# A two-block transformer kernel: 27 groups of 2x2 blocks of the down-projections made with seven block products instead of eight

## What is computed

```python
def sq_relu_mlp(h, w1, w2):
    return jnp.square(jax.nn.relu(h @ w1)) @ w2
...
    up = causal_dwconv(h @ w_up[l], conv_w[l], conv_b[l])
    y = (jax.nn.gelu(up[..., :D_FF_2], approximate=True) * up[..., D_FF_2:]) @ w_down[l]
    x = x + rms_norm_2(y, post_ffn_g[l])
```

## Time and profile before

| | |
|---|---|
| runs | 2095.36 us median (2094.35 to 2097.16) |
| profiled execution | 2095.49 us, span 2093.8 us |
| granted TensorE clock | 0.999 |
| TensorE busy | 2083.5 us, 9304 matmul records |
| TensorE weight loads | 1728.1 us, beside the matmuls |
| VectorE busy | 1224.2 us |
| ScalarE busy | 1072.2 us |
| POOL busy | 119.7 us |
| HBM read | 432.75 MB, 223 GB/s with the writes |

### The profile page before, as it was taken

The page is one execution under the profiler, slowest core; times in us unless marked ns, Lnnn a source line. Parts: engine busy times, 40 slices in busy tenths (PEclk is TensorE's granted clock), DMA queues, the critical chain, the costliest instruction groups (busy, mean ns, idle before and its releaser), DMA issues.

```text
span 2093.8 us, 23749 instructions
## 1 busy us (share of the span) xinstructions
PE 2083.5 (100%) x9304; PEld 1728.1 (83%) x9304; DVE 1224.2 (58%) x1312; ACT 1072.2 (51%) x1303; POOL 119.7 (6%) x66
## 2 busy tenths in 40 slices
PE   9999999999999999999999999999999999999998
PEld 8888888888888888888888888888888888888887
DVE  6546556655554555455566755566666654566665
ACT  7555654555434543455455554455555533555553
POOL 3000000000000000000002000000112100011120
PEclk9999999999999999999999999999999999999999
DMA  8688666888667885688588777667878766787863
GB/s 297 197 251 236 191 188 216 260 248 235 211 193 206 241 254 194 196 243 238 192 270 232 229 244 232 197 203 211 249 236 250 220 211 193 223 247 242 251 221 121
DMA packets 291903, 469.46 MB, mean 224 GB/s; under 512 B 18512, under 2 KB 82128, under 8 KB 291280
## 3 DMA queue, kind: packets, MB, share of 16 engines
q1 hardware_dynamic: 290928, 463.46, 72.5%
q10 hardware_dynamic: 864, 4.49, 0.6%
HBM read 432.75 MB, written 35.13 MB: 223 GB/s over the span
## 4 chain that ended last, share of the span: by engine, by line
PE 96%; DVE 1%; DMA 1%; ACT 1%; issue 0%; SPq 0%; ACTq 0%; DVEq 0%
PE ps L1546 96%; DMA T<-passed_strip 1%; DVE Wl L1204 0%; DVE zs L1416 0%; ACT Wh L986 0%; DMA E<-passed_rows 0%; DVE T L1256 0%; DMA gains<-in_gains_dram 0%; DVE E L1416 0%; ACT zs L1125 0%; SPq L917 0%; DMA passed_rows<-xN 0%; ACT T L1044 0%; DVE aHL L1307 0%; PE ps L1549 0%
## 5 line engine op out<-in xcount | busy, mean ns | idle before, releaser
L1204 DVE TENSOR_TENSOR Wl<-raw,Wh 128x1024 fp32r<-128x1024 f32 x743 | 908.2, 1242 | 674.2 <-ACT Wh L986 673.6
L1546 PE MATMUL ps<-Wh,aHL 128*128 128x512 f32 x3712 | 1148.8, 390 | 2.4 <-DVE Wl L1204 0.8
L986 ACT ACTIVATE Wh<-raw 128x1024 fp32r<-128x1024 f32 x743 | 768.0, 1054 | 611.1 <-PE ps L1546 608.7
L1546 PEld LDWEIGHTS ps<-Wh,aHL 128*128 128x128 f32 x3712 | 696.8, 188 | 147.9 <-DVE Wl L1204 1.3
L1546 PE MATMUL ps<-Wl,aHL 128*128 128x512 f32 x1856 | 722.1, 389 | 0.0
L1546 PE MATMUL ps<-Wh,hid 128*128 128x512 f32 x1728 | 532.8, 389 | 0.0
L1546 PEld LDWEIGHTS ps<-Wl,aHL 128*128 128x128 f32 x1856 | 348.4, 188 | 71.8
L1546 PEld LDWEIGHTS ps<-Wh,hid 128*128 128x128 f32 x1728 | 324.3, 188 | 67.4
L1546 PE MATMUL ps<-Wl,hid 128*128 128x512 f32 x864 | 336.1, 389 | 0.0
L1546 PEld LDWEIGHTS ps<-Wl,hid 128*128 128x128 f32 x864 | 162.2, 188 | 33.7
L1546 PE MATMUL ps<-Wh,oHL 128*128 128x512 f32 x512 | 159.0, 390 | 0.0
(11 more groups left out here) (167 smaller groups left out, 687.4 us busy)
## 6 DMA issues: line engine op xcount, KB each, us to landing
raw<-in_mlp_w_dram SPq DMA_DIRECT2D x256, 512.0 KB, 4.5
raw<-in_w_up_dram SPq DMA_DIRECT2D x176, 512.0 KB, 4.6
raw<-in_sb_w_qkv_dram SPq DMA_DIRECT2D x93, 512.0 KB, 5.2
raw<-in_w_down_dram SPq DMA_DIRECT2D x88, 512.0 KB, 4.7
raw<-in_w_in_dram SPq DMA_DIRECT2D x64, 512.0 KB, 4.8
passed_strip<-T SPq DMA_DIRECT2D x104, 256.0 KB, 4.5
T<-passed_strip SPq DMA_DIRECT2D x208, 128.0 KB, 5.2
raw<-in_sb_w_o_dram SPq DMA_DIRECT2D x32, 512.0 KB, 5.4
```

The costliest lines, as they stand in the source:

```text
L986: e.activation(Wh[:, i % NW, :], rawv[:, i % NRAW, :], ACT.Copy).then_inc(st["hi"][0], 1)
L1204: e.tensor_tensor(Wl[:, i % NW, :], rawv[:, i % NRAW, :], Wh[:, i % NW, :].bitcast(F32), ALU.subtract).then_inc(st["lo"][0], 1)
L1546: return e.matmul(o, l, r, start=start, stop=stop, skip_group_check=True)
```

## The change

In 15 places of the first block's down-projection and 12 of the second's, a 2x2 block of weights (two K tiles, even and odd, of two neighbouring strips a and b) and the matching 2x2 block of tokens (rows 0 and 1, even and odd tile) are multiplied by a Winograd form of Strassen's method: seven block products for eight. A group stands in the list as four pieces, s0 to s3, of two, two, two and one products (6, 6, 6 and 3 matmuls), in place of two pieces of 12. Only s0 and s1 load weights. Four sums of weights are made on VectorE (`weight_sums`), two of them then split as s2 and s3. Four sums of tokens are made once per pair of tiles, three pairs a chunk (`mix_tokens`, `mix_low`), into a new buffer hidMix. Four of the seven products, summed over the chunk's three groups, gather in ps2, three go straight to ps0 and ps1; at the pair's end `fold` and `fold_rest` add the four banks into the rows.

The first group comes after 4 plain pieces (2 in a pair without a tail), with 3 plain pieces between groups (2 in the second pairs of the chunks of five). The last pair of the first block has none. The first block's tokens now carry r before the square (a scale in the relu), so its sums are added plainly. In the second block the hid halves are planned 3 pieces on instead of 2.

```diff
+        b[0]["first"], b[0]["start"] = False, (False, True)
+        lead, gap = (4, 3) if tail else (2, 3 if len(plain) > 7 else 2)
+        rest = a[lead:n] + b[:n] if tail else a[lead:n - 1] + b[:2] + a[n - 1:] + b[2:]
+        p.pieces[first:] = a[:lead]
+        for m, kp in enumerate(sevens):
+            seven(w, s4, kp, mov, tiles, (a[0]["strip"], b[0]["strip"]), koff, m, m == 0, fold if m == len(sevens) - 1 else None)
+            p.pieces += rest[gap * m:gap * m + gap] if m < len(sevens) - 1 else rest[gap * m:]
+        p.pieces += a[n:] + b[n:] if tail else []
...
+    def mix_tokens(mov, src, k, n, need):
+        d = [done("token_mixed") for c in range(4)]
+        hi, lo = done("mixed_hi"), done("mixed_lo")
+        step("mix_tokens", mov=mov, src=src, k=k, n=n, need=[*need, *free["sums"]], d=d, hi=hi)
+        free["sums"] = [lo]
+        later(1, lambda: step("mix_low", mov=mov, k=k, n=n, hi=hi, lo=lo))
...
-            trip(s, k, n, "relu", None, [], landed)
+            trip(s, k, n, "relu", "b", [st["r2"]], landed)
...
                     step("gate_halves", t0=t0, need=[g, *k], hi=hi, lo=lo)
                     free["E"] = [lo]
+                    if t0 < 8:
+                        free["E"] = [lo, mix_tokens("hid2", "E", t0 // 2, 2 if t0 == 0 else 1, [g])]
...
-                later(2, halves)
+                later(3, halves)
...
+        q, n = p.pieces[i], int(p.pieces[i]["kind"][1])
+        if n == 0:
+            made = {m: done("weights_added") for m in (1, 3, 2, 4)}
+            step("weight_sums", a=raw_of[i] % NRAW, b=raw_of[i + 1] % NRAW, need=[landed(i), landed(i + 1), *free["sums"]], made=made)
+            free["sums"] = [(lo_sem, i + 4)]
+            for m in (1, 2, 3):
+                p.pieces[i + m]["made"] = made[(3, 2, 4)[m - 1]]
+        step("split", i=i, part=q["kind"], slot=raw_of.get(i, 0) % NRAW, loaded=landed(i) if n == 0 else q["made"],
+             used=(mm_sem, i - NW + 1), hi=(hi_sem, i + 1), lo=(lo_sem, i + 1))
+        if i in raw_of:
+            load(raw_of[i] + NRAW)
...
+                elif k == "weight_sums":
+                    e.tensor_tensor(wsum[:, 0, :], a[:, 0, :], b[:, 0, :], ALU.add).then_inc(made[1][0], 1)
+                    e.tensor_tensor(b[:, 0, :], b[:, 0, :], b[:, 1, :], ALU.add).then_inc(made[3][0], 1)
+                    e.wait_ge(*made[1])
+                    e.tensor_tensor(wsum[:, 1, :], wsum[:, 0, :], b[:, 1, :], ALU.add).then_inc(made[2][0], 1)
+                    e.wait_ge(*made[2])
+                    e.tensor_tensor(wsum[:, 2, :], wsum[:, 1, :], a[:, 1, :], ALU.add).then_inc(made[4][0], 1)
...
+            def seven_products(q):
+                terms = {"s0": (("a11", side[:, 0, :], q["opens"], True), ("a12", a[:, 0, :], False, False)),
+                         "s1": (("d1", side[:, 2, :], q["opens"], True), ("d3", b[:, 0, :], q["opens"], False)),
+                         "s2": (("d0", side[:, 1, :], q["opens"], True), ("d2", side[:, 3, :], q["opens"], True)),
+                         "s3": (("a22", a[:, 1, :], False, False),)}[q["kind"]]
+                for t, (name, P, starts, ends) in enumerate(terms):
+                    c = slice(t * 512, (t + 1) * 512)
+                    x, h, l = halves_of[name]
+                    mm(P, x[:, h:h + 128], wh[:, c], starts, False)
+                    mm(P, x[:, h:h + 128], wl[:, c], False, False)
+                    m = mm(P, x[:, l:l + 128], wh[:, c], False, ends and q["closes"])
```

231 lines of the change are left out of this document (178 added, 53 removed).

## The result

The changed kernel takes **2122.43 us** (median of 4 runs, 2117.78 to 2124.08) where the kernel before takes 2096.26 (4 runs, 2094.35 to 2098.72): 1.0121 times as long, 95% interval 1.0100 to 1.0141. 2097.0 had been forecast, with a range up to 2102.5. The profiled execution is the shortest of the four, 2117.78 us, span 2116.0. It is 22.2 us longer than the span before (2093.8), although TensorE has 81 matmuls fewer.

What follows compares the result with a forecast made beforehand. TensorE was taken as the bound, busy 2083.5 of 2093.8 us. Terms of -18.4 + 14.3 + 4.6 + 0.5 + 0.4 = +1.4 us gave 2097.0 us, range 2089.5 to 2102.5.

Steps and rivals of the forecast that it cites:

- the starts of the second block: From its down-projections' first piece (T0), piece 16's remainder comes 7.6 and 6.7 us late: 14.3 us, bounds 10.3 and 15.4.
- mixing: Second block's up-projections: token sums ahead of a strip's turn cost 3.45 us, two more places 0.6 each: 4.6, bounds 2 and 6.
- the remainder behind it is 4 us early: A fold falls where plain pieces follow, so the next remainder on VectorE is still 4 us ahead of need.
- the last down-projection: Squares of a finished strip stand on ScalarE before a group's third piece, 0.4 us late; bounds 0 and 2.
- saving: 27 groups make 21 matmuls of 24 each: 81 fewer at 0.2267 us, 18.4 us, all on the path.
- rival 2: The clock falls in the new gaps at the second block's down-projection starts: 8.6 us more, 2105.6 us; chance 0.25.
- first block's down-projections: At their three starts piece 11's remainder is 0 to 1.0 us late: 0.5 us for the three, bounds 0 and 3.
- A group among others costs nothing: Groups between plain pieces: VectorE's added sums fit, with a least cover of 2.2 us.
- That the halves come one piece later changes nothing here: it is POOL they wait for: Second block's down-projection starts: planning the halves 3 pieces on adds nothing to the chain from turn to piece 16.
- rival 1: The reload comes sooner and the second block's waits shrink: 2090.3 us; with everything hidden 2077; chance with everything hidden 0.25.
- the likeliest case: The forecast itself, 2097.0 us, within 0.2% of no change; chance 0.50.

Runs made afterwards that it cites:

- experiment 7: Changed kernel cut to 20 groups: none in the second block's tail pairs, two in the first block's third chunk; mixing 6 pieces behind halves at 2: 2093.15 us.
- experiment 12: Kernel of experiment 10 (17 groups) with halves 2 pieces on instead of 3 and mixing 7 pieces behind them instead of 6: 2085.22 us.
- experiment 10: Kernel of experiment 9 (18 groups) with two groups instead of three in the very last pair, so 17 groups: 2086.50 us.
- experiment 4: Changed kernel, all 27 groups, with the second block's token mixing planned 6 pieces after the halves: 2108.65 us.
- experiment 11: Kernel of experiment 4 with the weight sums of the second block's groups made over 8 columns instead of 512: 2102.0 us.
- experiment 3: Changed kernel without the second block's groups; the first block's 15 groups, token mixing and later halves stay: 2103.4 us.
- experiment 2: Kernel of experiment 1 with the three groups of the first block's third chunk back in, so 15 groups: 2090.17 us.
- experiment 1: Changed kernel with only the 12 groups of the first block's chunks 1 and 2; no second-block groups or mixing, halves 2 pieces on: 2087.01 us.
- experiment 8: Kernel of experiment 7 with one more group in each tail pair of the second block, behind 8 and 7 plain pieces: 2109.59 us.
- experiment 9: Kernel of experiment 7 without the first block's third-chunk groups, halves at 3 and mixing 6 behind, so 18 groups: 2087.91 us.
- experiment 13: Kernel before the change with only the second block's halves 3 pieces on instead of 2, no group, no mixing: 2096.29 us.

## Why the prediction was wrong

The profiled span was to grow by 1.4 us and grew by 22.2. Four terms of the sum were too small: the starts of the second block (the last strip's reload was taken to go out at T0 + 12.0, and POOL's product to keep its length), mixing (costed at three places), the first block's third down-projection ("the remainder behind it is 4 us early"), and the last down-projection (the bank, and the fold ahead of the last rounding). The table has the terms of the sum. A wait is a distance of two matmul starts over 0.62 us, less 0.227, and the row of the clock is the excess of the shorter distances:

| term | forecast | measured |
|---|---|---|
| saving | -18.4 | -18.4 |
| waits at the two starts in the second block | 14.3 | 15.9 (7.9, 8.0) |
| matmuls at the lower clock, there and behind | 0 (rival 2: 8.6) | 8.2 (2.3, 3.7, and 2.2 from 2057 on) |
| mixing in the up-projections | 4.6 | 8.0 (6.7, 1.25) |
| first block's down-projections | 0.5, at the starts | 3.8, at the end of the third |
| rest of the last down-projection | 0.4 | 4.6 |
| sum | 1.4 | 22.1 |

**The saving** and **"A group among others costs nothing"** were right. Two down-projections of the first block show it (18 matmuls fewer, 4.08 and 4.05 us), and so do second pairs of the second block where nothing else is in the way: 1.9 and 1.7 us for 9 matmuls in the first down-projection of experiments 7 and 12, 1.4 us for 6 in the last one of experiments 10 and 12.

**The starts of the second block** were right in mechanism: TensorE waited before pieces 11, 12 and 16, for a chain of fixed length. Their size was not, since waits and slow matmuls together made piece 16 later than forecast. Times from T0, first and second down-projection:

| | forecast | measured |
|---|---|---|
| reload issued | 12.0, 10.9 | 13.6, 14.3 |
| from there to the turn | 8.9 | 9.3, 10.2 |
| turn to the end of piece 16's remainder | 17.9 | 18.5, 18.4 |
| TensorE late at piece 16 | 7.6, 6.7 | 10.1, 11.7 |

(By the prediction's own steps the second is 6.5, not 6.7; the difference is small.) The step that failed is the first row. The chain was started too early: the convolution of the strip before was put at T0 + 7.0, as in the trace of before, and ended at T0 + 8.3 and 9.0; the reload stands behind it, by way of piece 5's remainder. The step "That the halves come one piece later changes nothing here: it is POOL they wait for" hid 1.1 us of that in each: POOL's product for the strip before is itself 1.13 us longer for the remainder that now stands ahead of the halves. The last strip's product is longer by 0.6, which is the third row. A wait before piece 4 (1.3 and 1.95 us) was not looked for either: the four sums stand ahead of that piece's remainder, whose cover had been 2.7 us in the first. From the reload's issue to the turn it took 19.5 us in both together, for 18.9 in the earlier trace rows, against rival 1.

**Rival 2, the clock, happened**, at both starts and once more at 2057. But its excess of 8.2 us is not its price. Of it 5.9 us (2.2 and 3.7) ran ahead of the two pieces 16, and those remainders were done 18.4 to 18.5 us behind the turn at all six such starts (the changed kernel, experiments 4 and 11), whether the slow matmuls ahead had cost 1.3 or 3.9 us. TensorE came to piece 16 with its remainder just done (cover 0.06 and 0.05 us), so at full clock it would have waited there instead. What the clock can have cost the span is by this estimate 8.2 - 5.9 = 2.3 us, nearly all of it behind 2057; no run here has these waits with the clock held up. The prediction let such a wait absorb 1.8 us a start, too little. The clock's fall itself was the consequence to expect, given the two waits of some 3 us each with 1.4 us of work between that the prediction derived, and the one row at hand (idle 2.26 us, clock still 1.00 and then 0.60) did not speak against it. So the likeliest case was worth less than its 0.5. Rival 2's 2105.6 would have been nearer, but by a price that was mostly not there, and still 12 us short of the profiled execution.

**Mixing** was costed right where it was looked at (3.45 at the turn) and then as two further places of 0.6. Six waits came in the first chunk, since the cover in these up-projections was down to 1.1 to 2.1 us at each of the next strips too, not at one alone, and every strip starts from a chain that is already late. Experiment 3 puts mixing and halves at 12.2 us in the up-projections alone (against experiment 2), and experiments 4 and 12 show that the whole is a matter of place.

**The first block's third down-projection** was worked out at its start, where the remainder of piece 11 kept 0.44 us of cover (0 to 1.0 late had been forecast), and not at its end. The alternation of VectorE and ScalarE for the norms was in the trace of before, with a cover that fell from 8.3 to 2.1 us; "the remainder behind it is 4 us early" (behind the fold) was taken as harmless, when it was the cover that this stretch lives on. Experiment 2 against 1 shows the loss, 2.0 us net, though 1.1 of its 3.2 us of waits are at the stage's start. That start, forecast as 0 to 1.0 late for each chunk, was on time in all three chunks of the changed kernel and late by 1.1, 1.0 and 3.0 us in the third chunk of experiments 2, 7 and 8: that it was on time here is in part luck.

**The last down-projection**: the squares ahead of a group were seen, but not that a pair's first group already waits for the neighbour strip's bank, behind 2 pieces of the pair where plain pieces open it behind 10, and behind a fold (2.3 us), nor that the last fold delays the last rounding (1.6). Experiment 10 shows the second by removing it. The first is absent in experiments 7, 9, 10 and 12, where the second pair has groups and no fold stands ahead of it; that fits, but it was not tried alone.

What stays open: the second start's chain began 3.0 us later against T0 than before (the turn of the strip before at T0 + 0.3 for T0 - 2.7), of which 1.1 is POOL's. Its other part varies between kernels that are the same up to there (T0 - 0.03 with 18 groups, T0 - 1.16 with 17), so it is at least partly a matter of when the reload lands; no run here separates it from mixing's. Nor is it known what makes the other three executions of the changed kernel 3.6 to 6.3 us longer than the profiled one.

## What to carry to other kernels

Before adding work to an engine that feeds the bottleneck, list the cover of every piece through the program, not the idle time of the engine: VectorE was 58% busy and had room for all the sums, and still the same mixing, with the later halves, cost 8 us in one place and nothing six pieces on. A place that is costed as late must be followed to the end of its stage (what starts from it, what alternates with it, and whether the waits that it makes bring the clock down), and a saving should be put only where the cover has come back: 17 groups of the 27 give 0.54% where all 27 lose 1.2%. The best version here is the one of experiment 12, 2085.2 us.

## What had not been expected of the hardware

**POOL's product takes as long as VectorE lets it.** 128x1024 elements took 5.58 us with three remainders of VectorE beside it and 6.71 with four. Less 1.14 us for each remainder that is 2.16 and 2.15 us: as though POOL stood still while VectorE made its remainders (both read two tiles). Counted by the overlap in the traces, POOL's time less VectorE's beside it is 2.2 to 2.3 us in 154 of the 165 products of all 15 profiles. It can go the other way: in eight of them POOL took 5.58 us, and it was the fourth remainder, begun 0.0 to 0.3 us behind the third, that took 3.0 to 3.4 us for its 1.23 and ended 1.1 behind POOL. Experiment 13's POOL and VectorE:

```profile
1829.74 5.58 POOL L1529 TENSOR_TENSOR E<-E,zs 128x1024 f32<-128x1024 f32 x1 [163.58 <-DVE E L1416]
...
1833.40 3.01 DVE L1204 TENSOR_TENSOR Wl<-raw,Wh 128x1024 fp32r<-128x1024 f32 x1 [0.33 <-ACT Wh L986]
```

The Trainium skill, page "SBUF — State Buffer", section "SBUF: two separate sides", has it that the two engines share a port pair, and that a VectorE operation with two inputs in SBUF or a GpSimd one, whichever starts first, keeps it for its whole instruction while the other is blocked. The trace agrees both ways, with 1.13 us more for POOL and 1.8 us more for VectorE. "It waits for POOL anyway" is thus no cover for more VectorE work beside it.

**The clock fell in or behind waits of 1.8 to 7.2 us**, for 3.4 to 10.2 us at a time, and not behind each. Experiment 8 waited 2.8 us at 990 and read 1.00, and the kernel of experiment 3 waited 2.1 us and, 4 us later, 1.4 us, and read 1.00 throughout (its window, columns as above):

```profile
1440.00:1475.00 35.00, 30.19 (x130) 1.00 0.76 208
```
